# HGRN diagonal scores in an encoder block: a summed product and eight column sums in place of eight score blocks

## The reference, cut to what matters

```python
def step(s_st, inp):                       # one chunk, one direction
    qc, kc, vc, fc = inp
    bcum = jnp.cumsum(fc, axis=-2)
    rel = bcum[:, :, :, None, :] - bcum[:, :, None, :, :]
    dec = jnp.exp(jnp.where(causal, rel, -jnp.inf))
    att = jnp.einsum('bhtk,bhtsk,bhsk->bhts', qc, dec, kc)
    oc = jnp.einsum('bhts,bhsv->bhtv', att, vc) + jnp.einsum('bhtk,bhkv->bhtv', qc * jnp.exp(bcum), s_st)
```

## Time and profile before

| | before |
|---|---|
| median of three executions | 2550.45 us |
| the profiled execution, its own time | 2551.23 us |
| its span from first to last instruction | 2549.5 us |
| TensorE busy | 2527.5 us, 99% of the span |
| VectorE busy | 1636.8 us, 64% |
| ScalarE busy | 914.8 us, 36% |
| GpSimd busy | 745.4 us, 29% |

### The profile page before, as it was taken

How to read it: one execution, slowest core, us unless ns; L and a number is a source line. 1 busy time by engine, 2 the same in 40 slices (tenths; PEclk the granted TensorE clock), 3 DMA queues, 4 the chain that set the end, 5 groups by cost and what they waited for, 6 DMA issues and landing times.

```text
span 2549.5 us, 33564 instructions
## 1 busy us (share of the span) xinstructions
PE 2527.5 (99%) x13158; PEld 2157.2 (85%) x13158; DVE 1636.8 (64%) x1864; ACT 914.8 (36%) x1122; POOL 745.4 (29%) x713
## 2 busy tenths in 40 slices
PE   9999999999999999999999999999999999999998
PEld 9888888889999999997888888876788888888887
DVE  6675555248888888866555424433457998887567
ACT  6342222133333333332323423333333443333433
POOL 2032232002121121234442001177413456553001
PEclk9999999999999999999999999999999999999999
DMA  8323333432223323344443536156414233225755
GB/s 294 121 96 108 99 127 105 140 140 92 84 100 108 107 93 116 108 150 140 165 149 145 201 125 215 34 192 208 155 49 149 85 114 131 101 99 194 276 191 182
DMA packets 181628, 349.67 MB, mean 137 GB/s; under 512 B 10459, under 2 KB 106023, under 8 KB 181472
## 3 DMA queue, kind: packets, MB, share of 16 engines
q1 hardware_dynamic: 119520, 154.44, 18.3%
q0 software_dynamic: 33088, 118.51, 13.3%
q10 hardware_dynamic: 28864, 74.59, 8.0%
HBM read 241.16 MB, written 106.33 MB: 136 GB/s over the span
## 4 chain that ended last, share of the span: by engine, by line
PE 96%; DMA 2%; DVE 1%; ACT 0%; issue 0%; POOL 0%; SPq 0%; ACTq 0%; DVEq 0%; POOLq 0%
PE ps L2301 18%; PE ps L2851 13%; PE ps L2440 12%; PE ps L2869 8%; PE ps L2332 7%; PE ps L2681 7%; PE ps L2507 4%; PE ps L2819 3%; PE ps L2464 3%; PE ps L2590 3%; PE ps L2611 2%; PE ps L2629 2%; PE ps L2379 2%; PE ps L2534 2%; PE ps L2522 1%; PE ps L2792 1%
## 5 line engine op out<-in xcount | busy, mean ns | idle before, releaser
L2301 PE MATMUL ps<-a_hi,whi 128*128 128x512 f32 x576 | 234.2, 407 | 0.0
L2301 PE MATMUL ps<-a_hi,wlo 128*128 128x512 f32 x576 | 224.8, 390 | 0.0
L2301 PE MATMUL ps<-a_lo,whi 128*128 128x512 f32 x576 | 224.4, 390 | 0.0
L1620 DVE TENSOR_TENSOR wlo<-raw,whi 128x2048 fp32r<-128x2048 f32 x59 | 135.8, 2302 | 114.4 <-ACT whi L997 113.3
L997 ACT ACTIVATE whi<-raw 128x2048 fp32r<-128x2048 f32 x59 | 113.1, 1917 | 190.4 <-PE ps L2681 105.1
L1002 ACT ACTIVATE ev<-ps 128x512 f32<-128x512 f32 x128 | 76.6, 599 | 208.0 <-PE ps L2301 131.2
L2332 PE MATMUL ps<-whi,a_hi 128*128 128x256 f32 x512 | 148.1, 289 | 0.0
L2332 PE MATMUL ps<-whi,a_lo 128*128 128x256 f32 x512 | 144.8, 283 | 0.0
L2332 PE MATMUL ps<-wlo,a_hi 128*128 128x256 f32 x512 | 144.7, 283 | 0.0
L793 POOL TENSOR_TENSOR cv<-cv,cs 128x1024 f32<-128x1024 f32 x16 | 38.5, 2404 | 322.6 <-ACT cs L1261 322.6
L2301 PEld LDWEIGHTS ps<-a_hi,wlo 128*128 128x128 f32 x576 | 108.1, 188 | 23.5
(11 more groups left out here) (422 smaller groups left out, 7197.1 us busy)
## 6 DMA issues: line engine op xcount, KB each, us to landing
raw<-in_w_in SPq DMA_DIRECT2D x45, 1024.0 KB, 6.6
raw<-in_w_up SPq DMA_DIRECT2D x22, 1024.0 KB, 5.1
hg_T<-ev ACTq DMA_DIRECT2D x32, 512.0 KB, 3.0
qfb<-hg_T POOLq DMA_DIRECT2D x24, 512.0 KB, 5.5
wd<-in_w_down POOLq DMA_DIRECT2D x44, 256.0 KB, 3.4
down_weight_sums<-wd POOLq DMA_DIRECT2D x22, 512.0 KB, 4.3
hidden_T<-ga ACTq DMA_DIRECT2D x11, 1024.0 KB, 4.0
hidden_sums<-s POOLq DMA_DIRECT2D x10, 1024.0 KB, 4.7
```

The source lines that it names most:

```text
L1620: signal(dve, dve.tensor_tensor(wlo[:, b.slot], w4[:, b.slot], whi[:, b.slot], ALU.subtract), w_lo, b.count())
L2301: ins = pe.matmul(ps[:, unit_bank(b, u)], W[sw][:, b.slot, k, c * P:(c + 1) * P], op[mw][:, k, t * HALF:(t + 1) * HALF], start=k == 0 and ...
```

## The change

It does three things in each of the 8 heads. VectorE multiplies the summed keys by the queries, in place, right behind the product that makes the queries, and raises `h_ksum` only then; TensorE no longer waits for `h_q` apart. TensorE multiplies each chunk of that product, as the stationary operand, by one column of ones, so that its 8 matmuls write one PSUM column each. ScalarE copies those 8 columns to a tile `diag` and then writes `Am` in 8 instructions, each of which scales the identity by one column of `diag`.

```diff
+        diag = sb("diag", [P, NT])
...
-                signal(act, act.activation(Am[:], psw[:, 2048:3072].rearrange("p (c t) -> p c t", c=NT), ACT.Copy),
-                       h_diag, h + 1)
+                line(act.activation(diag[:], psw[:, 2048:2048 + NT], ACT.Copy))
+                for c in range(NT):
+                    ins = act.activation(Am[:, c], ident[:], ACT.Copy, scale=diag[:, c:c + 1])
+                    if c < NT - 1:
+                        line.free(ins)
+                    else:
+                        signal(act, ins, h_diag, h + 1)
...
             def key_sums(h):
-                signal(dve, dve.tensor_tensor(Sall[:, 0].rearrange("p c v -> p (c v)"), Y[:, 0], Y[:, 1], ALU.add), h_ksum, h + 1)
+                line(dve.tensor_tensor(Sall[:, 0].rearrange("p c v -> p (c v)"), Y[:, 0], Y[:, 1], ALU.add))
...
                 signal(dve, dve.tensor_tensor(qs[:], qs[:], qfb[:, 0], ALU.mult), h_q, h + 1)
+                flat = Sall[:, 0].rearrange("p c v -> p (c v)")
+                signal(dve, dve.tensor_tensor(flat, flat, qs[:], ALU.mult), h_ksum, h + 1)
                 if step:
                     gate_result(h)
...
                 pe.wait_ge(h_ksum, h + 1)
-                pe.wait_ge(h_q, h + 1)
...
                 for c in range(NT):
-                    ins = pe.matmul(pair(0, c), chunk(Sall[:, 0].rearrange("p c v -> p (c v)"), c), chunk(qs, c), start=True, stop=True)
+                    ins = pe.matmul(psw[:, 2048 + c:2049 + c], chunk(Sall[:, 0].rearrange("p c v -> p (c v)"), c), ones[:, 0:1], start=True, stop=True)
```

## The result

| | before | changed |
|---|---|---|
| median | 2550.56 us (6 executions) | 2567.49 us (6 executions, 2563.73 to 2569.35) |
| the profiled execution | 2551.23 us | 2563.73 us |
| its span | 2549.5 us | 2561.8 us |

The change makes the kernel slower: the ratio of the times is 1.006 (95% interval 1.0051 to 1.0070), 16.9 us between the medians. The forecast was 2558.7 us, with a range up to 2561.5. The direction held; the size was twice what I gave it. The profiled execution is the fastest of the six, so it shows 12.3 us of the loss and not all of it.

A forecast was written before the change was run, and what follows sets the result against it. TensorE was taken as the bound. The late product's 1.26 us in head 1 and 7.0 us in heads 2 to 7, plus 0 for narrower matmuls and ScalarE, made 8.3 us on 2550.45: 2558.7 us, range 2554.5 to 2561.5.

The forecast's parts named there:

- What bounds the kernel: Whole span: TensorE, busy for 99%, is the bound; in the heads' stretch each microsecond it waits lengthens the program.
- The edge between two heads: From the last dense load to the diagonal's first load: queries are made exactly as late as TensorE can bear.
- 0.07 us of release: Head 1's diagonal: TensorE's first load starts 0.07 us after the end of VectorE's product that makes the queries.
- 0.09 us to spare: Head 2's diagonal: its first load could have gone at 700.31 and went at 700.40, leaving 1.17 us of wait.
- The added product: VectorE's new 1.26 us product before the diagonal: 1.26 us in head 1, 1.17 each in heads 2 to 7, 0 in head 0.
- The narrower matmuls: TensorE's 16 diagonal passes a head, one column for 128: gain taken as 0, at most 0.84 us a head.
- the pair of L2413: A plain 32-bit matmul in two passes moving 64 columns, starting 0.11 to 0.14 us apart: nearest row, so no gain.
- The rival of the clock: TensorE's clock falls in seven new waits of 1.2 us, adding over 10 us; chance 1%.
- ScalarE's nine instructions: Scaled identities before the level 1 keys: nine at 0.32 us, 2.9 us a head, 0.5 us left, cost 0.
- The other rivals: Load no bound, 2552.4 us (11%); ScalarE late, 2565 (6%); late release not holding TensorE, down to 2543.7 (2%).
- The range: Forecast's own 2556 to 2560 us; the 8-in-10 range, 2554.5 to 2561.5, adds half-way load pace and slightly late ScalarE.
- what I said the changed profile would show: Seven diagonal waits of 1.2 us, 16 loads in 1.7 to 1.8 us, head period 1.2 us longer, no level 0/1 waits.

The follow-up runs named there:

- the kernel that has the waits and no fall: The changed kernel with the diagonal's matmuls moving all 128 columns of ones again, late product and seven waits kept: 2559.70 us, ratio 1.0038.
- the first series: The changed kernel's first six executions, beside the kernel before: median 2567.49 us, ratio 1.006.
- the second: The changed kernel itself measured once more, beside the kernel before at 2551.09 us: 2565.57 us, ratio 1.0059.
- the run of the key sums: The changed kernel without the product by the queries, TensorE waiting for `h_q` as before; one-column matmuls and ScalarE's nine instructions stay: 2550.40 us, ratio 1.0000.

## Why the prediction was wrong, and where it was right

- **What bounds the kernel** held. The edge between two heads was the place that decides, and the 0.07 us of release and 0.09 us to spare that head 2 showed made a wait of 1.17 us; 1.14 were measured. Head 1 was overpriced a little: its diagonal starts 0.88 us later than before, not 1.26, as its queries came 0.36 us earlier (627.34 against 627.70 us).
- **The added product** was priced at 8.3 us. The waits of the loads sum to 7.5 us, and the kernel that has the waits and no fall is 8.8 us slower by its median. This term was right. In head 0 no load waits for the product, as said.
- **The narrower matmuls** were right as a duration and wrong as a cost. A pass takes 0.111 us with one column, against 0.1125; the pair of L2413 was the right neighbour. The Trainium skill, on its page "TensorE: Matmul & The Clock Gate", section "LDWEIGHTS (loading the stationary operand)", puts a load of 128 columns at 107 ns. The pace of 0.111 us in this trace agrees with it. The 25 ns that the same page's section "Back-to-back issue gap" gives for 1 to 64 columns do not show here, where each matmul has a load of its own. That the load is what sets the pace is not shown, as no run changed the load of these passes; that the moving side does not is shown. But "I take 0 for the gain" stopped at the block's own length. That one-column passes behind a wait bring falls of TensorE's clock, where passes with 128 columns behind the same wait bring none, was in no term of the sum, and this is the step that failed: the narrower matmuls were put at a cost of 0, and their falls account for 4.9 us of the profiled span (2561.8 - 2556.9). In the medians what is above the waits is 7.8 us in the first series and 5.7 in the second, of which a part stays open.
- **The rival of the clock** was there, at 1%, with the wrong condition. I hung it on the waits alone. The run with waits alone shows no fall; with one-column matmuls behind the waits three or more of seven heads fall. Its price was near: over 10 us for all seven heads is some 1.4 us a fall, and 1.3 to 1.6 were measured. What it had wrong is when a fall comes, and in how many heads.
- **ScalarE's nine instructions** cost nothing that shows: 0.61 us were left before the level 1 keys, and the run of the key sums stands at the time of the kernel before. A scaled copy is 389 ns long and starts (2.45 - 0.39) / 7 = 0.29 us after the one before, the lower bound of my 0.29 to 0.40.
- **The other rivals** are out. The passes got no shorter; ScalarE is not late; the late release does hold TensorE.
- **The range** took in only the terms I had. Of what I said the changed profile would show, the waits, the length of the passes and the levels without a wait came out right. The head's period did not: I had it 1.2 us longer, and in three heads it is 2.7 us longer (74.1 against 71.4). That row is where the loss shows, and a row of the clock in short stretches gives its cause.

Two things stay open. Why a given head falls and its neighbour with the same instructions does not (heads 1, 3, 6 in one execution, 2, 4, 6 in another) was not settled. And about 2 us of the slower executions of the changed kernel is explained neither by the waits nor by the number of falls that their granted clock allows.

## What to carry to other kernels

Where TensorE is full, ask of every edit that puts idle time or very narrow matmuls on it what it does to the engine's clock, and not only how long it takes; then look at the granted clock in stretches of 2 to 4 us, because the page's slices hide a fall of 3.4 us, and compare the mean granted clock of every execution, as a profile is only one of them. A narrower moving side saved nothing in 32-bit passes that each load a 128x128 block (0.111 us against 0.1125), so look for fewer passes. And before an instruction is put ahead of a signal, read by how much the waiting engine is late or early at that signal now: here 0.09 us, so the whole product was exposed, and one dense piece issued ahead of the wait covers it.

## What the runs showed of the hardware

I had not expected that TensorE can be without a single wait (583.00 us busy of 583.00) and see its granted clock fall to 1.2 GHz for 3.4 us: in three of the heads with 16 passes that move one column, where the same kernel with 128 columns shows no fall, and in six heads with 32 such passes. In the records these passes look much like the others: 0.25 us long against 0.28 with 128 columns, and as before one every 0.11 us. A wait of 1.1 us brought no fall with wide matmuls, a wait of 2.3 us brought five in seven heads. Nor had I expected that the number of falls differs from execution to execution of one kernel, with the scatter of 5.6 us that the changed kernel has.
